# A transformer block on one core: last conditioning weights in a home of their own, narrow products among wide ones, ten unused products in the router's chain

## The reference

```python
def _ec_moe(h, w_router, w_gate, w_up, w_down):
    cap = EC_FACTOR * L // N_EXPERTS                       # 32
    aff = jax.nn.softmax((h @ w_router).astype(jnp.float32), axis=-1)
    vals, idx = lax.top_k(jnp.swapaxes(aff, 1, 2), cap)
    xs = h[bidx, idx]
    hid = jax.nn.silu(jnp.einsum('becd,edf->becf', xs, w_gate)) * jnp.einsum('becd,edf->becf', xs, w_up)
    y = jnp.einsum('becf,efd->becd', hid, w_down) * vals[..., None]
    return jnp.zeros_like(h).at[bidx, idx].add(y)
...
x = x + mod_x[2] * merge(o_x, g_x, hy_x)
x = x + channel_mix(x, mod_x)        # mod[5] * _ec_moe(modulate(rmsnorm(x), mod[3], mod[4]))
```

## Time and profile before

| | before |
|---|---|
| time, median of 3 runs | 1532.47 us (1532.1, 1532.47, 1546.83) |
| the profiled execution, its own time | 1544.27 us |
| its span, first to last instruction | 1542.4 us |
| PE / DVE / ACT / POOL busy, share of the span | 84% / 41% / 32% / 7% |
| read from memory | 373.55 MB, 243 GB/s over the span |
| chain that ended last | PE 64%, DMA 26%, DVE 3%, ACT 3% |

### The profile page before, as it was taken

The page is one execution under the profiler, slowest core; times in us unless marked ns, Lnnn a source line. Parts: engine busy times, 40 slices in busy tenths (PEclk is TensorE's granted clock), DMA queues, the critical chain, the costliest instruction groups (busy, mean ns, idle before and its releaser), DMA issues.

```text
span 1542.4 us, 22551 instructions
## 1 busy us (share of the span) xinstructions
PE 1298.7 (84%) x9326; PEld 964.6 (63%) x9326; DVE 637.5 (41%) x941; ACT 498.1 (32%) x756; POOL 107.3 (7%) x117
## 2 busy tenths in 40 slices
PE   5999999785555555656599999999999999999997
PEld 2388667431101101211286999999999987999997
DVE  2624746310100100100377665566545548566554
ACT  2425414310000000000237543445343438544443
POOL 0010110100000000000028000000000008000000
PEclk8999999798887877777799999999999999999999
DMA  9532736979999999999841466555566751355662
GB/s 368 194 98 80 249 134 268 417 309 420 417 421 419 418 421 419 420 420 419 325 155 56 128 199 188 167 178 173 185 196 184 212 156 57 97 177 163 192 201 70
DMA packets 137965, 376.69 MB, mean 244 GB/s; under 512 B 9422, under 2 KB 56959, under 8 KB 137702
## 3 DMA queue, kind: packets, MB, share of 16 engines
q1 hardware_dynamic: 137894, 375.68, 67.1%
HBM read 373.55 MB, written 1.05 MB: 243 GB/s over the span
## 4 chain that ended last, share of the span: by engine, by line
PE 64%; DMA 26%; DVE 3%; ACT 3%; SPq 1%; POOL 1%; issue 1%; ACTq 0%; DVEq 0%
PE psum L1930 16%; PE psum L1932 15%; PE psum L1931 15%; DMA ring<-in_w_up 6%; DMA work<-in_w_gate 6%; PE psum L2260 3%; DMA ring<-in_w_down 3%; DMA work<-in_w_down 3%; DMA tokens<-in_w_down 3%; PE psum L1866 2%; DMA ring<-in_w_ada 2%; DMA early<-in_w_gate 1%; DMA ring<-in_w_gate 1%; PE psum L2109 1%; SPq L572 1%; POOL work L756 1%
## 5 line engine op out<-in xcount | busy, mean ns | idle before, releaser
L1930 PE MATMUL psum<-parts 128*128 128x256 f32 (+1 forms) x1672 | 496.5, 297 | 12.1 <-DVE parts L1578 9.9
L1931 PE MATMUL psum<-parts 128*128 128x256 f32 (+1 forms) x1672 | 494.2, 296 | 0.0
L1932 PE MATMUL psum<-parts 128*128 128x256 f32 (+1 forms) x1672 | 494.0, 295 | 0.0
L1572 DVE TENSOR_TENSOR parts<-ring,parts 128x1024 fp32r<-128x1024 f32 x232 | 280.8, 1227 | 169.6 <-ACT parts L1040 168.9
L1930 PEld LDWEIGHTS psum<-parts 128*128 128x128 f32 x1672 | 321.5, 192 | 22.9 <-issue 14.3
L1932 PEld LDWEIGHTS psum<-parts 128*128 128x128 f32 x1672 | 321.6, 192 | 7.3
L1931 PEld LDWEIGHTS psum<-parts 128*128 128x128 f32 x1672 | 321.6, 192 | 7.2
L1040 ACT CAST parts<-ring 128x1024 fp32r<-128x1024 f32 x232 | 239.6, 1045 | 249.2 <-PE psum L1932 208.0
L2260 PE MATMUL psum<-ring,work 128*32 128x512 f32 x512 | 82.4, 778 | 71.7 <-DMA ring<-in_w_up 36.1
L1030 ACT ACTIVATE work<-psum 128x1024 f32<-128x1024 f32 x4 | 4.1, 1024 | 381.8 <-PE psum L2260 381.8
L2260 PE MATMUL psum<-work 128*32 128x512 f32 x512 | 84.8, 805 | 42.9 <-DMA work<-in_w_gate 24.5
(11 more groups left out here) (353 smaller groups left out, 1407.4 us busy)
## 6 DMA issues: line engine op xcount, KB each, us to landing
ring<-in_w_qkv_b SPq DMA_DIRECT2D x72, 512.0 KB, 4.3
work<-in_w_gate SPq DMA_DIRECT2D x16, 2048.0 KB, 22.9
ring<-in_w_up SPq DMA_DIRECT2D x16, 2048.0 KB, 23.4
ring<-in_w_ada SPq DMA_DIRECT2D x48, 512.0 KB, 8.5
work<-in_w_down SPq DMA_DIRECT2D x12, 2048.0 KB, 23.1
ring<-in_w_gate SPq DMA_DIRECT2D x44, 512.0 KB, 4.3
ring<-in_w_up SPq DMA_DIRECT2D x44, 512.0 KB, 5.2
ring<-in_w_down SPq DMA_DIRECT2D x44, 512.0 KB, 4.3
```

What stands on the lines that cost most here:

```text
L1572: dve.tensor_tensor(part_of(lo_slots, t, n), ring[:, slot_2(t), 0:n], part_of(hi_slots, t, n), ALU.subtract).then_inc(lo_ready, 1)
L1930: pe.matmul(out, lhsT[0], rhs[0], start=start, stop=False, skip_group_check=True)
L1931: pe.matmul(out, lhsT[0], rhs[1], start=False, stop=False, skip_group_check=True)
L1932: return pe.matmul(out, lhsT[1], rhs[0], start=False, stop=stop, skip_group_check=True)
```

## The change

It has three parts.

First, ada5's last four tiles (84 to 87) get a home of their own, `late`, which is work[0:4096], instead of ring slots 4 to 7. They raise `ring_full` 8 to 11, which tiles 80 to 83 used before them, so SP waits for the landing of those. They are issued right after `y_ready`, ahead of the quads. `homes` is put in another order: home 2 is now ring 4-7, home 3 ring 0-3, home 4 ring 8-11, home 5 work[0:4096].

Second, on PE ada3 moves behind the second inverse transform (and to banks 4 and 5), and mod(2, 3) moves between the two output groups. ACT's copy for it moves behind `squares_o(0)`.

Third, `keep_busy(n)` issues n products of 512 columns whose result in bank 7 nobody reads: five before the wait for `top_done`, three before `pick_ready`, two before `pick_taken`.

```diff
--- before.py
+++ after.py
@@ -425,7 +425,7 @@
         part("w_out", [k_tiles(w_out, 0, D)[k] for k in OUT_ORDER])
         part("ada5", k_tiles(w_ada, 5 * D, 6 * D))
 
-        ADA_BANK, MOD_BANK, GATE_BANK = [6, 6, 4, 0, 0, 2], [5, 5, 0, 0], (4, 2)
+        ADA_BANK, MOD_BANK, GATE_BANK = [6, 6, 4, 4, 0, 2], [5, 5, 0, 0], (4, 2)
         X_BANK, LOGIT_BANK = 4, 0
 
         T_MOE = len(stream)
@@ -438,13 +438,18 @@
         assert T_IN % SLOTS == 0
 
 
-        slot_1 = [t % SLOTS if t < T_IN else TURNS[EG + (t - T_IN) % SLOTS_1] if t < T_OUT else TURNS[(t - T_OUT) % SLOTS] for t in range(T_MOE)]
+        slot_1 = [t % SLOTS if t < T_IN else TURNS[EG + (t - T_IN) % SLOTS_1] if t < T_OUT else TURNS[min(t - T_OUT, (t - T_OUT) % EG + 2 * EG)] for t in range(T_MOE)]
         fills_1 = [slot_1[:t + 1].count(slot_1[t]) for t in range(T_MOE)]
 
         before_1 = [max((i + 1 for i in range(t) if slot_1[i] == slot_1[t]), default=0) for t in range(T_MOE)]
         before_1[T_OUT:T_OUT + EG] = [upto_tile["hy1"]] * EG
         full_counts = [slot_1.count(i) for i in range(SLOTS)]
         t = upto_tile["ada3"]
+        late = cut(0, EG, 1024)
+
+        def weight(t):
+            return late[:, t - (T_MOE - EG), :] if t >= T_MOE - EG else ring[:, slot_1[t], :]
+
         load_order = [*range(t), *range(T_OUT, T_OUT + EG), *range(t, T_OUT), *range(T_OUT + EG, T_MOE - EG)]
 
 
@@ -460,8 +465,8 @@
         fulls = [(full, 0) for full in moe_full] + [in_ring(i)[1:] for i in TURNS_2[2 * EG + 1:3 * EG]] + [(ctx_loaded, 16)]
         more = [(slots_of, full, before) for slots_of, (full, before) in zip(ring_moe, fulls, strict=True)]
 
-        homes = [*more[0:3], *(in_ring(TURNS_2[EG * i]) for i in (2, 0, 1)), *more[3:]]
-        HOMES, RING_HOMES = len(homes), (4, 5, 3)
+        homes = [*more[0:2], *(in_ring(TURNS_2[EG * i]) for i in (1, 2, 0)), *more[2:]]
+        HOMES, RING_HOMES = len(homes), (4, 2, 3)
         BRIEF, TOKENS = HOMES - 2, HOMES - 1
         assert BRIEF < 2 * KD
         turns = [r for r in range(HOMES) if r != BRIEF]
@@ -543,9 +548,11 @@
             sp.dma_start(consts[:, :], d["c_ident"]).then_inc(net_loaded, 16)
             def load_weight(t):
                 src, n = stream[t]
-                if t >= SLOTS:
+                if t >= T_MOE - EG:
+                    sp.wait_ge(ring_full[slot_1[t]], 16 * fills_1[t] - 16)
+                elif t >= SLOTS:
                     sp.wait_ge(tiles_done, before_1[t])
-                sp.dma_start(ring[:, slot_1[t], 0:n], src).then_inc(ring_full[slot_1[t]], 16)
+                sp.dma_start(weight(t)[:, 0:n], src).then_inc(ring_full[slot_1[t]], 16)
 
             for t in load_order:
                 if t == upto_tile["ada1"]:
@@ -581,13 +588,13 @@
                 if q == 0:
                     sp.wait_ge(conv_out, 2)
                     sp.wait_ge(y_ready, 1)
-                elif q == RING_HOMES[2]:
                     for t in range(T_MOE - EG, T_MOE):
                         load_weight(t)
+                elif q == RING_HOMES[1]:
+                    sp.wait_ge(tiles_done, T_OUT + EG)
+                elif q == RING_HOMES[2]:
                     sp.wait_ge(tiles_done, T_OUT + KD)
                 elif q == RING_HOMES[0]:
-                    sp.wait_ge(tiles_done, T_OUT + KD + EG)
-                elif q == RING_HOMES[1]:
                     sp.wait_ge(tiles_done, T_MOE)
                 elif q == TOKENS:
                     sp.wait_ge(logits_ready, 1)
@@ -966,9 +973,9 @@
                     act.copy(sblk[64:P, 2 * dr:2 * dr + 2, c, DV:2 * DV],
                              state[64:P, (n + 1) % 2, 2 * dr:2 * dr + 2, :]).then_inc(sblk_act, 1)
             row(3)
-            mod(2)
             split_out(0)
             squares_o(0)
+            mod(2)
             act.wait_ge(o_ready, 2)
             act.wait_ge(conv_out, 2)
             act.copy(yT_parts[0][:, HEADS:KD, :], yT[:, HEADS:KD, :]).then_inc(y_taken, 1)
@@ -1845,7 +1852,7 @@
                 t = tiles[0]
                 tiles[0] += 1
                 pe.wait_ge(ring_full[slot_1[t]], 16 * fills_1[t])
-                return ring[:, slot_1[t], :]
+                return weight(t)
 
             def turn(src, ready, bank=0):
                 for k in range(KD):
@@ -2146,20 +2153,20 @@
             to_spectrum(1)
             update(6)
             to_spectrum(3).then_inc(u_ready, 1)
-            ada(3, 0, 8)
             pe.wait_ge(state_ready, 14)
             scores_gla(0)
             scores_gla(1)
-            mod(2, 3)
-            pe.wait_ge(mod_taken, 3)
             from_spectrum(1, 0)
             from_spectrum(1, 1)
+            ada(3, 0, 8)
             pe.wait_ge(scT_ready, 2)
             pe.wait_ge(sblk_ready, 8)
             pe.wait_ge(sblk_act, 8)
             out_gla(0)
+            pe.wait_ge(conv_out, 2)
+            mod(2, 3)
             out_gla(1)
-            pe.wait_ge(conv_out, 2)
+            pe.wait_ge(mod_taken, 3)
             ada(4, 0, 8)
 
             def mixed(i, w, t):
@@ -2216,20 +2223,31 @@
                                     start=(i == 0 and t == 0), stop=(i == KD - 1), skip_group_check=True)
             ins.then_inc(logits_ready, 1)
             turn(xres, xt_ready, X_BANK)
+
+            def keep_busy(n):
+                for i in range(n):
+                    pe.matmul(ps[7].rearrange("p (k l) -> p k l", k=4), xn_parts[:, 0, 0, 0], xn_parts[:, 0:4, 0, 0, :],
+                              start=True, stop=True)
+
             pe.wait_ge(aff_ready, 1)
             for t in range(TT):
                 ins = pe.transpose(ps[1][0:EXPERTS, P * t:P * t + P], aff[:, t], ident[:, :])
             ins.then_inc(aff_turned, 1)
             gate(5)
+            pe.wait_ge(xn_hi_ready, 1)
+            pe.wait_ge(xt_taken, 6)
+            keep_busy(5)
             pe.wait_ge(top_done, 1)
             for i in range(2):
                 ins = pe.matmul(ps[LOGIT_BANK][:, NG * i:NG * i + NG], spread2[:, i], spread[:, P:P + NG], start=True, stop=True)
             ins.then_inc(slots_ready, 1)
+            keep_busy(3)
             pe.wait_ge(pick_ready, 1)
             for g in range(NG):
                 for t in range(TT):
                     ins = pe.transpose(ps[t][:, P * g:P * g + P], pickT[:, g, P * t:P * t + P], ident[:, :])
             ins.then_inc(pick_turned, 1)
+            keep_busy(2)
             pe.wait_ge(pick_taken, 1)
             pe.wait_ge(gate_taken, 2)
             pe.wait_ge(xt_taken, 6)
```

## The result

The changed kernel takes **1530.06 us** (median of 20 executions, 1525.72 to 1534.81); the kernel before, in as many beside it, 1536.78 (1532.10 to 1546.83). The ratio is 0.9946, 95% interval 0.9931 to 0.9961: 8.3 us faster, with an interval of 6.0 to 10.6. One execution of the kernel before, beside a later experiment, took 4186.72 us and is left out of all that follows.

What follows compares the result with a forecast made beforehand. The expert weight-load stream was taken as the bound: its 10.0 us stall plus a 3.07 us earlier start gave a 13.1 us gain, from the 1532.47 us median to 1519.4 us, range 1515 to 1530 us.

Steps and rivals of the forecast that it cites:

- fourth case: Expert stage: the permuted homes slow the expert weight stream, making the kernel slower, 1539 us; chance 0.04.
- last line of the sum: Whole kernel: the 13.1 us gain taken from the median of 1532.47 us, giving 1519.4 us.
- fifth case: Whole kernel: moved clock phases may add to the runs' 12 to 14 us step, gain over 15.3 us, 1515 us; chance 0.15.
- Term (1): PE order around the second inverse transform: full clock, no wait, earlier ada4 and stream start, -3.07 us; -0.3 if clock falls.
- Term (2): ada4's loads, issued about 225.0 instead of 215.33 us, still land in time: cost nothing, cover 1.2 us.
- Term (3): Last ada5 tiles loaded ahead of the quads: the turn of normed tokens starts 5.41 us earlier and runs 0.6 us shorter.
- Term (4): Quads 2 to 5 change homes: the load stream gets no gap, cost nothing.
- Term (5): Ten unused products between router and gather keep PE's clock full: -3.4 us if it holds, 0 if not.
- second case: Router chain: the clock falls despite the unused products, gain only 9.5 to 10.3 us, 1522.5 us; chance 0.22.
- first case: Main forecast: clock holds, PE reaches the first quad at 304.0 us, stream never stops, gain 13.1 us; chance 0.49.

Runs made afterwards that it cites:

- b_copy2: The kernel before, unchanged but for a comment, profiled again; one execution, 1544.11 us.
- x_fill: The kernel before with only the ten unused products added; median 1538.82 us, ratio 0.9985.
- b_up: The kernel before with three unused products put before the gate input products at 119 us; median 1537.26 us, ratio 0.9995.
- b_copy: The kernel before, unchanged but for a comment, run again for its spread; median 1538.38 us, ratio 1.0002.
- b_copy3: The kernel before, unchanged but for a comment, profiled once more; one execution, 1539.19 us.
- x_late_fill: The kernel before with the late tiles' home, home order and unused products, without the new PE order; median 1532.22 us, ratio 0.9951.
- y_q0: The changed kernel with the first quad's load issued before ada4's tiles; median 1530.80 us, ratio 0.9948 to the kernel before.
- y_up: The changed kernel with three unused products at 119 us and ten instead of five before the top-k's end; 1527.63 us, ratio 0.9930 to before.

## Why the prediction was wrong in size and right in mechanism

**The stream's stall was the bound, and it went.** In the profiled pair the experts end 13.26 us sooner (756.34 to 743.08), for 13.1 forecast: 3.50 from the start of the stream (3.07 forecast) and 9.76 from the stall (10.0 forecast). 0.96 us is given back in the second block, which leaves the span's 12.3. The thin stretch of 310 to 330 us has gone, and from 330 us on the rate is the 419 GB/s of before, so the fourth case (permuted homes) is out. x_late, which has the tiles' home and the order of homes alone, brings 7.5 of the 8.3 us by itself.

**The step that failed is the last line of the sum: "against the median the forecast is 1519.4 us".** There a gain was subtracted that had been measured on one execution of the upper group (1544.27) from a median of the lower group (1532.47). I wrote that the execution lay 11.8 us above the median "for a reason that I don't see in this stage". It was in this stage, at least in part: in the two profiles of the lower group the transform already runs at full clock, the stall is 6 and 8 us, and the experts end at 746.95 and 748.15 us instead of 756.34. Against the changed kernel's 743.08 that is 4 to 5 us to win, not 13. From the groups' means the changed kernel's mean of 1530.3 is 14.1 us less than the upper (1544.4) and 6.1 less than the lower (1536.4). Weighted by 33 and 47 that is 9.4; the means of the pair's own executions, side by side, differ by 9.0. In figures: of the 10.66 us by which the forecast was low, 4.31 are the median itself (1532.47 of three executions, 1536.78 of twenty), and the rest is the gain. The fifth case saw the step of 12 to 14 us between the runs and took it for extra gain; it was the base's own, and cut the other way.

**Term (1), order, -3.07.** Right in the pair: the transform took 7.16 us at clock 1.00 instead of 9.96, the wait is gone, and from the 16 records at 193 us to S it is 3.37 us less. But 2.81 us of the term hang on a clock that stands at half in only four of the eight profiles with the old order (before, b_copy2, x_fill, b_up; not b_copy, b_copy3, x_late, x_late_fill). Where it stands at full, the order is worth 0.2 us. The term should have carried a chance of about a half.

**Term (2), ada4's loads, 0.** Right. They were issued at 224.93 us, and ada4's second half did not wait.

**Term (3), late tiles, -5.41 and -0.6.** Right, and by x_late nearly the whole gain over all executions. The turn began at 272.03 us, 8.80 sooner; forecast were 8.48. DVE is what is late next, as foreseen (the turn waits 1.09 us for it).

**Term (4), home order, 0.** Right: no gap at 251 or 271 us. y_q0 shows how near it is: with one quad less, there is one.

**Term (5), unused products, -3.4 if the clock holds.** It did not: the clock was at half from 289 to 295 us. This is the event of the second case, yet PE reached the first quad at 304.00, as the first case said. Three things paid for it. The logits took 3.72 us instead of 5.66, because the clock now fell only near their end (0.83 from 278 to 279 us); the turn took 1.97 instead of 2.70; and the clock rose three products into the gather instead of ten, 1.25 us. From turn to first quad 12.49 - 8.80 = 3.69 us were won, and the forecast had 4.0 from (3)'s 0.6 and (5). So the forecast of 304.0 us for the first quad, met to the hundredth, was luck: the sum was right by other addends. My argument that one stand of 1.4 us would be borne rested on the length of a stand, and that does not decide it: in the changed kernel PE stood 1.24 us ahead of the fall, but 1.51 us before the first quad, behind which the clock stayed at 1.00, and in y_q0 it fell with no stand at all.

**The rule on transposes.** The prediction took the trace's side against the Trainium skill (TensorE: Matmul & The Clock Gate, "Part 4: PE-mode transpose"), by which the full clock doesn't engage in transpose mode. In y_up the eight transposes take 1.09 us at a granted clock of 1.00, 1.97 us in the changed kernel at 0.50: here they do run at the full clock, and the measurement decides.

## What to carry to other kernels

When the runs of a kernel are spread in two groups, find out first which group the profile is from, by its own time, and subtract a gain only from a time of that group: a sum may be right to 0.2 us and the forecast off by 10. When two edits shorten the same stall, the first takes most of it and the other is paid only what is left; look for what else is nearly as late (here homes, PE and bytes) before moving one of them further. Whether unused products hold the clock has to be read from a trace and can't be had from the length of the hole: five failed in all four profiles, with a stand behind them or without, and ten held in both.

## What the runs showed of the hardware

**Falls of the clock come or don't come from execution to execution, at set places of the program.** Beside those at 120 us and in the transform there are two in the second block. In b_copy3 they are at 1077 to 1087 and 1267 to 1277 us:

```profile
1077.00:1087.00 10.00, 8.45 (x60) 8.40 (x59) 7.71 (x8) 2.10 (x2) 0.00 (x0) 0.83 0.45 158
...
1267.00:1277.00 10.00, 9.42 (x120) 6.99 (x122) 6.01 (x21) 6.38 (x20) 5.67 (x6) 0.83 0.01 2
```

Their price shows in the time from E to the end, in all 14 profiles. Taken over the same two hundreds of microseconds behind E (300 to 400 and 500 to 600), the clock is 1.00 and 1.00 where the rest of the program takes 785.8 to 786.1 us, 0.98 and 1.00 where it takes 786.9 to 787.5, and 0.98 and 0.98 where it takes 788.6 to 789.4. The pair's 0.96 us that were given back go with one such fall; since b_copy and b_copy3 have two of them with the code of the kernel before, I take it for no effect of the change. What decides whether a fall comes stays open. Of the five profiles with 0.66 at 120 us three have no fall in the second block and two have one; of the eight with 1.00 there, three have one and five have both. A kernel that stops all of them was not tried.

**The stall's size goes with the clock in the router's chain.** b_copy2 is 5.7 us later than b_copy3 at S and 9.5 us later at E. The 3.8 us more arise behind S: from S to the eleventh quad it is 75.11 us in one and 71.40 in the other, at a mean granted clock of 0.84 and 0.88. The logits alone take 5.75 us in b_copy2 and 3.71 in b_copy3. Whether an early fall brings the later ones, or only goes along with them, isn't shown.
